# A two-layer mixture-of-experts encoder: two more ring units for expert weights, and the last down matrices by halves of columns

## The reference

```python
for e in range(N_EXPERTS):                              # 32 experts, D = 1024, F = 256
    he = jax.nn.silu(xt @ w_gate[e]) * (xt @ w_up[e])   # each 1024 x 256: 1 MB
    out = out + gates[:, e:e + 1] * (he @ w_down[e])    # 256 x 1024: 1 MB
...
y = h * lax.rsqrt(mean(h * h) + NORM_EPS) * norm_final  # after the second layer, real tokens only
```

## Time and profile before

| | us |
|---|---|
| median of 3 runs | 745.19 |
| lowest and highest | 743.14, 747.56 |
| span of the profiled execution | 743.9 |
| TensorE busy in it | 645.1 (87%) |
| VectorE, ScalarE, GpSimd busy | 252.9, 175.9, 63.6 |
| bytes moved by DMA | 233.85 MB, 314 GB/s over the span |

### The profile page before, as it was taken

One profiled execution on the slowest core, in us unless ns is written; L12 is line 12 of the kernel. 1 busy time (PEld: TensorE's weight loads), 2 busy tenths in 40 slices (PEclk: granted clock), 3 DMA queues, 4 the chain that ended last, 5 costly groups with the idle time before them and its releaser, 6 DMA issues.

```text
span 743.9 us, 11131 instructions
## 1 busy us (share of the span) xinstructions
PE 645.1 (87%) x4744; PEld 402.6 (54%) x4744; DVE 252.9 (34%) x586; ACT 175.9 (24%) x359; POOL 63.6 (9%) x55
## 2 busy tenths in 40 slices
PE   3999999997899999599679999998899897676774
PEld 3898988355557474265224345677656363244331
DVE  5166344124132324022124388923313221211213
ACT  5554340022101010000003347833211010000002
POOL 4222270000000000000000550000000000000000
PEclk9999999997999999999889999999899998879888
DMA  9751434993899999999998305059999999999992
GB/s 299 278 181 47 156 99 157 365 422 132 330 423 366 422 420 425 421 422 422 416 410 329 135 36 163 9 198 424 403 397 422 422 420 424 421 422 423 420 412 81
DMA packets 46042, 233.85 MB, mean 314 GB/s; under 512 B 4480, under 2 KB 4736, under 8 KB 23456
## 3 DMA queue, kind: packets, MB, share of 16 engines
q1 hardware_dynamic: 45152, 232.34, 78.1%
q0 software_dynamic: 832, 0.70, 0.7%
HBM read 231.96 MB, written 1.05 MB: 313 GB/s over the span
## 4 chain that ended last, share of the span: by engine, by line
PE 63%; SPq 18%; DMA 12%; DVE 4%; issue 2%; ACT 1%; DVEq 0%; ACTq 0%
SPq L382 11%; PE bank L1807 9%; DMA ring<-in_moe_w_down 8%; SPq L385 6%; PE bank L1871 6%; PE bank L1895 5%; PE bank L1844 5%; PE bank L1509 5%; PE bank L1511 4%; PE bank L1510 4%; PE bank L1858 4%; PE bank L1959 4%; PE bank L1713 4%; DMA ring<-in_moe_w_up 4%; PE bank L1967 2%
## 5 line engine op out<-in xcount | busy, mean ns | idle before, releaser
L1807 PE MATMUL bank<-ring,hnT 128*32 128x256 f32 (+1 forms) x1624 | 138.1, 451 | 46.3 <-DMA ring<-in_moe_w_up 23.4
L1807 PEld LDWEIGHTS bank<-ring,hnT 128*32 128x32 f32 x1624 | 70.0, 126 | 107.0 <-issue 46.6
L1895 PE MATMUL bank<-moe_scratch 128*128 128x512 f32 (+1 forms) x160 | 78.5, 615 | 1.7 <-ACT moe_scratch L775 1.6
L1250 DVE TENSOR_TENSOR h<-bank,h 128x512 f32<-128x512 f32 (+1 forms) x80 | 55.1, 689 | 44.5 <-PE bank L1895 44.5
L1844 PE MATMUL bank<-ring,moe_scratch 128*32 128x512 f32 x448 | 62.1, 624 | 0.3 <-ACT moe_scratch L771 0.3
L1509 PE MATMUL bank<-hnT_hi,mix_hi 128*128 128x272 f32 x192 | 58.2, 303 | 1.7 <-DVE scratch L1092 1.7
L1871 PE MATMUL bank<-sel,hn 128*128 128x256 f32 x240 | 59.2, 406 | 0.0
L1871 PEld LDWEIGHTS bank<-sel,hn 128*128 128x128 f32 x240 | 58.1, 337 | 0.0
L1511 PE MATMUL bank<-hnT_lo,mix_hi 128*128 128x272 f32 x192 | 56.6, 295 | 0.0
L1510 PE MATMUL bank<-hnT_hi,mix_lo 128*128 128x272 f32 x192 | 56.5, 294 | 0.0
L1267 DVE TENSOR_TENSOR moe_scratch<-moe_scratch,bank 128x256 f32<-128x256 f32 x16 | 6.7, 421 | 145.1 <-ACT moe_scratch L769 145.1
(11 more groups left out here) (306 smaller groups left out, 882.0 us busy)
## 6 DMA issues: line engine op xcount, KB each, us to landing
ring<-in_moe_w_down SPq DMA_DIRECT2D x56, 1024.0 KB, 26.0
ring<-in_moe_w_gate SPq DMA_DIRECT2D x48, 1024.0 KB, 22.8
ring<-in_moe_w_up SPq DMA_DIRECT2D x48, 1024.0 KB, 24.0
ring<-in_sc_w_in SPq DMA_DIRECT2D x12, 1024.0 KB, 12.3
tail<-in_moe_w_up SPq DMA_DIRECT2D x7, 1024.0 KB, 26.9
tail<-in_moe_w_gate SPq DMA_DIRECT2D x7, 1024.0 KB, 25.9
tail<-in_moe_w_down SPq DMA_DIRECT2D x6, 1024.0 KB, 22.4
ring<-in_att_w_in SPq DMA_DIRECT2D x6, 1024.0 KB, 21.0
```

The costliest lines, as they stand in the source:

```text
L1250: nc.vector.tensor_tensor(hh, B[[7, 4][k % 2]][0:n, :], hh, ALU.add).then_inc(sem(f"h_added{l}"), 1)
L1807: return mm(bank[at, :], xT[:, c, mine], right, start=(c == 0), stop=(c == KC - 1))
L1895: mm(B[[7, 4][k % 2]][0:m, :], selgT[:, TILE_AT[t]:TILE_AT[t] + m], y[:, half, :], start=True, stop=True).then_inc(sem(f"sc_ps{l}"), 1)
```

## The change

1. `spare`, two more slots (16 KB per partition), is taken from SBUF; the space set aside for GpSimd's load descriptors is cut to 512 (`dynamic_dma_scratch_size=512`). The ring has 20 slots in layer 0 and 21 in layer 1. Units 18 and 19 of layer 0 load behind the fourth of the mixer's blocks, units 20 and 21 of layer 1 behind the last block of its mixer. The order of the slots changes with it, and the final gain goes to another slot.
2. GpSimd issues no loads any more: the first nine go to ScalarE ahead of the first norm, the 14 later ones to SyncE behind the fourth block, the copy for attention to SyncE too.
3. The last group's four down matrices are loaded as eight units of half the columns (0.5 MB each), first all first halves. `down` and `scatter` of the last group go by halves; both halves are stages of their own. The order of the last scatter is now halves outside and tiles inside, and the final squares follow it.
4. A sixth weight semaphore; two pairs of routing semaphores become one pair.

```diff
-    RING, HOME, SIDE = [18, 19], 16, 2
+    RING, HOME, SIDE, SPARE = [20, 21], 16, 2, 20
...
-        UNITS += [("d", 4 * q + j, 0) for j in range(4)]
+        if q < NQ - 1:
+            UNITS += [("d", 4 * q + j, 0) for j in range(4)]
+        else:
+            UNITS += [("half_d", 4 * q + j, half) for half in range(2) for j in range(4)]
...
-    RING_ORDER = [[16, 17, 8, 9, 10, 11, 0, 1, 2, 3, 4, 5, 6, 7, 12, 13, 14, 15],
-                  [18, 4, 5, 3, 8, 9, 10, 11, 12, 13, 14, 15, 6, 7, 16, 17, 0, 1, 2]]
+    RING_ORDER = [[0, 1, 2, 3, 4, 5, 6, 16, 17, 8, 9, 10, 11, 12, 13, 14, 15, 20, 21, 7],
+                  [18, 4, 5, 3, 8, 9, 10, 11, 12, 13, 14, 15, 6, 7, 16, 17, 0, 1, 2, 20, 21]]
...
+                elif kind == "half_d":
+                    cols = slice(half * W, half * W + W)
+                    src = A["moe_w_down"][l, e].rearrange("(p c) n -> p c n", c=2)[:, :, cols]
+                    sp.dma_start(dst.rearrange("p (c n) -> p c n", c=2)[:, :, cols], src)...
...
+                if 2 * b + 2 == MIX_RING:
+                    later_params()
+                    for i in (18, 19):
+                        unit(0, i)
...
             def first_units1():
+                sp.wait_ge(sem("stage_done0"), ...)
+                for i in (20, 21):
+                    unit(1, i)
+                sp.wait_ge(sem("kv_raw"), 3)
+                sp.dma_start(vm[32:32 + NM, 1, :], vm[0:NM, 0, :]).then_inc(sem("vm_in"), 16)
                 sp.wait_ge(sem("rstd_att"), 1)
                 unit(1, 1)
...
+            first_params()          # nine loads on ScalarE
             norm(0)
...
-                for k, (half, t) in enumerate(scattered(q, tiles)):
+                for k, half, t in scattered(tiles, halves):
...
-                    down(r, q)
-                    scatter(r, q)
+                    for half in range(2):
+                        down(r, q, (half,))
+                        scatter(r, q, (half,))
```

More of the change, by code:

```diff
@@ L78, in gate_up_stages, with down_stage @@
         return [3 * q, 3 * q + 1]
-    def down_stage(q):
-        return gate_up_stages(q)[-1] + 1
+    def down_stage(q, half=0):
+        return gate_up_stages(q)[-1] + 1 + (half if q == NQ - 1 else 0)
     def slot_of(l, i):
@@ L159, in build_program @@
         tail = sb("tail", [P, SIDE * UNIT])
+        spare = sb("spare", [P, 2 * UNIT])
         slots += [tail[:, i * UNIT:(i + 1) * UNIT] for i in range(SIDE)]
         slots += [rows[:, 2 * D:4 * D], moe_scratch[:, ONCE_AT:ONCE_AT + UNIT]]
+        slots += [spare[:, i * UNIT:(i + 1) * UNIT] for i in range(2)]
         gain_first = slots[HOME + 1][:, UNIT - D:UNIT]
-        gain_last = slots[RING_ORDER[1][8]][:, 0:D]
+        gain_last = slots[RING_ORDER[1][GAIN_AT]][:, 0:D]
         spent = [0]
@@ L389, in first_units0 @@
                 sp.wait_ge(sem("proj_ps"), PROJ["ac"] + 4)
-                for i in (7, 8):
+                for i in (1, 2):
                     unit(0, i)
                 sp.wait_ge(sem("proj_ps"), PROJ["ab"] + 4)
-                for i in (9, 10, 1, 2):
+                for i in (3, 4, 8, 9):
                     unit(0, i)
@@ L397, in first_units0 @@
                 sp.wait_ge(sem("ya_ready"), 4)
-                for i in (3, 4, 5, 6, 15, 16, 17, 18):
+                for i in range(10, 18):
                     unit(0, i)
                 wait_mix_read(sp, 0, NMIX[0] - 2)
-                for i in (11, 12):
+                for i in (5, 6):
                     unit(0, i)
@@ L482, in _ @@
             pool.wait_ge(sem("pool_step"), 2)
[L483 to L492, removed]
             pool.wait_ge(sem("w_g_in"), 16)
@@ L498, in _ @@
                 low_mix(pool, nc.gpsimd, 0, u)
[L499 to L508, removed]
             pool.wait_ge(sem("featT_ps"), 1)
@@ L533, in wait_h, with scattered @@
             else:
-                eng.wait_ge(sem(f"h_added{n // 2 - 1}"), steps * NQ * 2 * tiles + (NQ - 1) * 2 * tiles + 2 * (i + 1))
-        def scattered(q, tiles):
-            if q < NQ - 1:
-                return [(half, t) for half in range(2) for t in tiles]
-            return [(half, t) for t in tiles for half in range(2)]
+                eng.wait_ge(sem(f"h_added{n // 2 - 1}"), steps * NQ * 2 * tiles + (NQ - 1) * 2 * tiles + tiles + i + 1)
+        def scattered(tiles, halves=(0, 1)):
+            return [(half * len(tiles) + i, half, t) for half in halves for i, t in enumerate(tiles)]
         def wait_hnT(eng, n):
@@ L589, in norm @@
                     done = steps * NQ * 4 + (NQ - 1) * 4
-                    for i, t in enumerate(tiles):
-                        for half in range(2):
-                            act.wait_ge(sem("h_added1"), done + 2 * i + half + 1)
+                    for half in range(2):
+                        for i, t in enumerate(tiles):
+                            act.wait_ge(sem("h_added1"), done + 2 * half + i + 1)
                             cols = slice(half * W, half * W + W)
@@ L1297, in last_group @@
                     groups(r, (NQ - 1,))
-                    add_tokens(r * NQ, NQ - 1)
+                    add_tokens(r * NQ, NQ - 1, (1,))
                 all_but_last(0, True)
@@ L1834, in he_transposes, with down @@
                     last.then_inc(sem(f"heT_ps{l}"), 1)
-                def down(r, q):
-                    pe.wait_ge(sem(f"heT{l}"), r * NQ + q + 1)
-                    w = [slots[at] for at in arrived(r, down_stage(q))]
-                    for half in range(2):
+                def down(r, q, halves=(0, 1)):
+                    if halves[0] == 0:
+                        pe.wait_ge(sem(f"heT{l}"), r * NQ + q + 1)
+                    w = [slots[at] for at in arrived(r, down_stage(q, halves[0]))]
+                    for half in halves:
                         for c in range(2):
@@ L1882, in transpose_weights, with scatter @@
                     last.then_inc(sem(f"selgT_ps{l}"), 1)
-                def scatter(r, q):
+                def scatter(r, q, halves=(0, 1)):
                     pe.wait_ge(sem(f"selgT{l}"), r * NQ + q + 1)
-                    for k, (half, t) in enumerate(scattered(q, tiles)):
+                    for k, half, t in scattered(tiles, halves):
                         m = TILE_N[t]
```

69 lines of the change are left out of this document (47 added, 22 removed).

## The result

The changed kernel took 726.7 us in the median (723.48 to 727.71), the kernel before on the same chip 744.16: a ratio of 0.9762, with a 95% interval of 0.9729 to 0.9795. The forecast was 727.9. The profiled execution spans 724.8 us against 743.9.

What follows compares the result with a forecast made beforehand. The weight stream was taken to bound both expert layers, with TensorE's work after the last landing. Terms -9.9 + 1.7 - 5.3 - 4.3 + 0.5 = -17.3 us gave 727.9 us, own range 724 to 731 (chance 0.66).

Steps and rivals of the forecast that it cites:

- The sum: Whole kernel: all terms together, -17.3 us, taken from the median of the kernel before.
- the ring: Both expert layers: two more units already in SBUF save 4.97 us of transfer per layer, -9.9 us together.
- the two overlaps: Ends of both expert layers: work on first halves while second halves land, -5.3 and -4.3 us.
- the rows of 2 KB: Last four down matrices of each layer: shorter runs go at 389 instead of 422 GB/s, +0.85 us per layer.
- the moves: Small loads moved off GpSimd: ScalarE's nine early issues cost +0.5 us at the start, the later ones are covered.
- The bound: Both expert layers: they end when the last weight has landed, plus what TensorE then still has to do.
- The first layer's end: Layer 0, last landing to attention's transposes: 7.4 us instead of 12.7, so -5.3 us (bounds -3.5 and -7.1).
- On them, all at the low level: Layer 0's first halves: products, eviction and scatter at half clock take 7.3 us, reaching the second half 1.9 us late.
- The second layer's end: Layer 1, last landing to kernel end: 12.4 us instead of 16.8, so -4.3 us (bounds -2.6 and -5.3).
- The start: Before the first norm: ScalarE's nine load issues delay TensorE's start by 0.5 us (bounds 0 and +2.5).
- Rival (a): First 20 us: ScalarE's queue moves each short run by itself at 53 ns, +5 us, 732.9 us; chance 0.18.
- The step that was costed at nothing: Behind layer 0: attention's later weight blocks follow at 5.4 us each, costed at 0; a late one would show once.

Runs made afterwards that it cites:

- the ring alone: Kernel before with the small loads moved, two more ring units per layer, new slot order and sixth semaphore, last down matrices whole: 735.36 us, ratio 0.9874.
- the moves alone: Kernel before with only the small loads moved to ScalarE and SyncE and GpSimd's load scratch cut: 745.08 us, ratio 1.0024.
- the halves not used: Changed kernel, but TensorE waits for both halves of the last down matrices and scatters after all 16 products: 734.23 us, ratio 0.9863.
- split parameters: Changed kernel with gla_gain and conv_w loaded behind the gate's first copy, on a semaphore waited for later: 725.9 us, ratio 0.9756.
- late parameters: Changed kernel with only w_g_in loaded ahead of the first norm, the other eight small loads right behind it: 733.14 us, ratio 0.9866.
- a scatter put first: Changed kernel with the scatter of the last group but one moved ahead of the last group's gate products: 727.15 us, ratio 0.9777.
- the last kernel: Changed kernel with split parameters and the earlier scatter of the last group but one together: 723.67 us, ratio 0.9734.

## Why the prediction was right, step by step

**The sum: right, and in part by luck.** Forecast -17.3 us, measured -17.7 by the ratio. The parts that the experiments could price are the ring with -11.2 us (the ring alone against the moves alone, where -9.9 was forecast), the two overlaps with -7.5 to -8.0 (-9.6), the rows of 2 KB with -0.8 (+1.7) and the moves with +1.8 (+0.5). Each of them is uncertain by some 2 to 4 us on either side, so none of the four contradicts its term. But two came out lower than their terms and two higher, and that the sum agrees within 0.4 us is more than such terms can promise.

**The bound: right.** The stream sets the expert layers. Two more units took 9.4 us off, by the ratio, with nothing else changed at the ends (the ring alone, with its late start in it), where -9.9 plus the start's +0.5 was forecast. In the changed kernel's trace TensorE's last wait for gate matrices in the first layer ends 4.5 us earlier than before (361.60 against 366.10), although the early part was 0.4 us later: -4.9 for one layer, against a term of -4.97.

**Rows of 2 KB: right as a rate, invisible as a time.** 387 to 404 GB/s in the windows above, forecast 389. The price that this has in the time, forecast as 0.85 us a layer, can't be seen between the ring alone and the halves not used (a difference of 0.0011 the other way, with some 0.005 on either side). The Trainium skill ("DMA: Bandwidth & Descriptors", Specifications) puts line rate at 512 B and up. The windows here show 2 KB runs 4 to 8% below runs of 8 KB, and for this stream the windows decide.

**The first layer's end: right in its sum, by two errors that nearly cancelled.** Forecast: landing at 383.6, transposes 7.4 us later at 391. Measured: 381.8, and 8.3 us, 390.15. The step with a wrong premise is "On them, all at the low level". The first half's products took 1.97 us, not 3.57: the clock did fall to 0.50 (1.2 GHz) behind the wait that ended at 361.60, but TensorE then worked nearly without a pause (3.95 of the 4 us from 364), and at 370 to 382 us it was granted 1.00 (2.4 GHz), where the earlier trace rows has 0.50 behind a wait for the down matrices themselves. The "On them" was wrong as well. The last of the first halves was issued at 359.19 and took 17.7 us:

```profile
ring<-in_moe_w_down SPq DMA_DIRECT2D x1, 512.0 KB, 17.7
```

It landed at 376.85, but the products began only at 378.69, because TensorE was still at the group's earlier work; the first half hadn't to be waited for at all. That start, 1.7 us later than the landing allows (0.14 us behind it in the forecast), and the products, 1.6 us shorter, cancel. TensorE came to the second half 2.5 us behind its landing (384.36 against 381.85), where 1.9 was forecast. I had the end follow from the landing; it follows from the gate matrices' landing at 361.60, by 28.55 us of TensorE's own work and the copies between, so products at the low clock would have put it 1.6 us later (an estimate).

**The second layer's end: right.** Landing forecast at 714.1, measured 712.94; 12.4 us forecast behind it, measured 11.9. Here TensorE had finished the first half's scatter (710.82 + 1.95 = 712.77) just ahead of the second half's landing, so the lateness of 1.0 us that I had put in wasn't there. Together the two overlaps were to be worth 9.6 us; the kernel that loads the halves but doesn't use them is 7.5 to 8.0 us slower than the changed one.

**The start: too small, and with a wrong order.** The prediction's "behind the table load, which ends at 2.01" was wrong: the table load comes after the loads. TensorE started at 11.39 in the changed kernel, where 11.3 was forecast, but that agreement is luck. In the profiles of kernels with this same start it ranged from 11.08 to 13.35. The moves alone measured +1.8 us (-0.2 to +3.8), against a term of +0.5 and bounds of 0 and +2.5.

**Rival (a): the premise right, the price wrong.** ScalarE's queue does move each short run by itself: it moved 2,836 packets for some 2,720 runs. ScalarE's queue in the changed kernel, 0 to 12 us, against the earlier trace rows:

```profile
q10 hardware_dynamic: 1728, 0.17, 11.6%
```

11.6% of 12 us x 16 engines is 22.3 us over 1,728 packets: 12.9 ns each, a quarter of the 53 ns that the rival was priced at. At that price all 2,836 take some 2.3 us of each engine (an estimate from this row), not 9.0. Where the same loads came 9 us later, with the stream full, they did hurt, as latency: 13.3 us for a load of 2 KB, and 7 us on the kernel. The kernel with split parameters issued the same three loads later still, at 22.7 us, where each took some 9.8 us, and lost nothing, for no product of that stage waited for them. What decides is when these loads are issued and who waits for them, which the rival left out.

**The step that was costed at nothing and wasn't nothing.** "The blocks behind it follow at 5.4 us each; I cost them at nothing." That is nearly true of the changed kernel, whose ring has its own order: ScalarE waits 2.3 us for attention's output blocks there, and that wait is not in the chain that ended last. In the old order of slots in a ring of 18 the halves lose 6.3 of their 8.5 us to attention's blocks. What the old order would cost in a ring of 20 no run shows. Extended by slots 20 and 21, it would put the second halves into slots 13, 14, 15 and 20 and the first halves into 5, 6, 7 and 12, so the third and fourth of attention's blocks would wait for the first halves' products and none for the last ones. My working gave the new order no term and no reason.

**What stays open.** How much of the start's spread is ScalarE's issues and how much the landing of the tokens; what the unprofiled runs with late parameters lost beyond the 4.7 us of the profiled one; what the rows of 2 KB cost in time; what fills the 4 us between TensorE's products and a scatter put first; whether the last kernel is faster than the changed one. The smaller scratch of GpSimd's queue was only run together with the moves.

## What to carry to other kernels

When a stream bounds a stage, price more buffer by its bytes, and the end of the stage by what TensorE has to do after the last landing; then check whether the end hangs on that landing or on an earlier one, because a shorter tail only pays until the earlier one is the bound. When units are added to a ring or split, work out for each slot who used it last and who is next: the gain of a split can be lost to a block that waits for a slot which the split has made the last to be free. In these runs small loads with short runs were best issued ahead of the point at which the stream fills up, and not counted on one semaphore with loads that are needed sooner (splitting them off changed both their place and their semaphore, so the two are not told apart). On ScalarE they stood in front of its first work; a queue whose engine has nothing urgent was not tried.

## What the runs showed of the hardware that I had not expected

The issue of the three conv_w loads (512 single elements each) held ScalarE for 1.7 to 4.0 us: 1.71 and 1.83 in the changed kernel's two profiles, 1.74, 1.99, 2.32, 3.55, 3.89, 4.00 and 4.03 in seven kernels with the same instructions up to there, and 1.60 when they were issued at 22.7 us. What decides isn't known. A table load stands behind the DMA issues that come ahead of its activation in the program, so that these delay it: it began at 0.73 us with no issue ahead, 1.44 with one, 3.43 with five and 5.80 with nine. Where TensorE reads a value and branches on it, 4.4 us passed in the first layer and 4.3 in the second in which no instruction is shown; a wait had hidden them. What of it is the read, the branch or a load of instructions isn't shown. The clock behind a wait differs between two executions of the same kernel: 0.50 and 0.78 granted at 360 to 364 and 364 to 368 us in the changed kernel's first profile, 0.74 and 0.84 in its second, each behind a wait for the gate matrices, and 1.00 in both at 370 to 382 us.
